# Order of the first two large loads of a decoder trunk: first weight slab ahead of the first norm's scale

## The reference

```python
def rms_norm(x, g):
    y = xf * lax.rsqrt(jnp.mean(xf * xf, axis=-1, keepdims=True) + EPS)
    return (y * g.astype(jnp.float32)).astype(x.dtype)

def swiglu_ffn(x, w_in, w_out):
    gate, up = jnp.split(x @ w_in, 2, axis=-1)
    return (jax.nn.silu(gate) * up) @ w_out

for i in range(DEPTH):
    x = x + 0.5 * swiglu_ffn(rms_norm(x, ffn1_norm[i]), ffn1_w_in[i], ffn1_w_out[i])
    xn = rms_norm(x, mix_norm[i])
    ...
    x = x + y
    x = x + 0.5 * swiglu_ffn(rms_norm(x, ffn2_norm[i]), ffn2_w_in[i], ffn2_w_out[i])
return rms_norm(x, final_norm)
```

## Time and profile before

| | before |
|---|---|
| median of 3 runs | 940.22 us (940.21 to 940.26) |
| span of the profiled execution | 938.5 us |
| TensorE, busy | 927.6 us (99%) |
| TensorE, weight loads | 872.2 us (93%) |
| VectorE, busy | 522.7 us (56%) |
| ScalarE, busy | 411.9 us (44%) |
| GpSimd, busy | 26.7 us (3%) |
| moved by DMA | 170.36 MB, 182 GB/s on average |

### The profile page before, as it was taken

One profiled execution on the slowest core, in us unless ns is written; L12 is line 12 of the kernel. 1 busy time (PEld: TensorE's weight loads), 2 busy tenths in 40 slices (PEclk: granted clock), 3 DMA queues, 4 the chain that ended last, 5 costly groups with the idle time before them and its releaser, 6 DMA issues.

```text
span 938.5 us, 15299 instructions
## 1 busy us (share of the span) xinstructions
PE 927.6 (99%) x6505; PEld 872.2 (93%) x6505; DVE 522.7 (56%) x464; ACT 411.9 (44%) x413; POOL 26.7 (3%) x44
## 2 busy tenths in 40 slices
PE   8999999999999999999999999999999999999997
PEld 7999999989989999999999999999999899999995
DVE  5765545446967665455547444554478475454533
ACT  6453334326744544333435344334364265343322
POOL 1500000000000000000000000000010000000000
PEclk9999999999999999999999999999999999999999
DMA  8985555523512875676518656556184277556501
GB/s 264 310 270 179 179 179 201 196 75 120 172 46 101 303 241 180 217 236 202 179 45 278 217 179 213 184 197 190 46 288 161 90 242 263 185 177 209 196 7 45
DMA packets 124213, 170.36 MB, mean 182 GB/s; under 512 B 2773, under 2 KB 108777, under 8 KB 124168
## 3 DMA queue, kind: packets, MB, share of 16 engines
q1 hardware_dynamic: 124168, 169.69, 54.1%
HBM read 168.63 MB, written 1.05 MB: 181 GB/s over the span
## 4 chain that ended last, share of the span: by engine, by line
PE 96%; issue 1%; DVE 1%; DMA 1%; ACT 1%; POOL 0%; SPq 0%; POOLq 0%; ACTq 0%; DVEq 0%
PE ub L894 10%; PE ub L896 10%; PE ub L895 10%; PE ga L894 10%; PE ga L896 10%; PE ga L895 10%; PE acc L894 10%; PE acc L895 10%; PE acc L896 10%; PE ga L1093 1%; PE tp L955 1%; DMA raw<-in_ffn_w_in_dram 1%; PE ub L1093 1%; PE tp L1180 0%; DVE w_lo L607 0%
## 5 line engine op out<-in xcount | busy, mean ns | idle before, releaser
L607 DVE TENSOR_TENSOR w_lo<-raw,w_hi 128x2048 fp32r<-128x2048 f32 (+1 forms) x154 | 352.1, 2295 | 246.3 <-ACT w_hi L410 246.1
L410 ACT ACTIVATE w_hi<-raw 128x2048 fp32r<-128x2048 f32 (+1 forms) x154 | 292.1, 1902 | 91.9 <-PE acc L896 61.5
L894 PE MATMUL ub<-xn_hi,w_hi 128*128 128x256 f32 x688 | 195.1, 284 | 0.0
L894 PE MATMUL ga<-xn_hi,w_hi 128*128 128x256 f32 x688 | 194.8, 283 | 0.2 <-ACT sgh L455 0.2
L896 PE MATMUL ub<-xn_hi,w_lo 128*128 128x256 f32 x688 | 194.7, 283 | 0.0
L895 PE MATMUL ub<-xn_lo,w_hi 128*128 128x256 f32 x688 | 194.7, 283 | 0.0
L896 PE MATMUL ga<-xn_hi,w_lo 128*128 128x256 f32 x688 | 194.7, 283 | 0.0
L895 PE MATMUL ga<-xn_lo,w_hi 128*128 128x256 f32 x688 | 194.7, 283 | 0.0
L894 PE MATMUL acc<-w_hi,act_hi 128*128 128x512 f32 x416 | 163.6, 393 | 0.0
L895 PE MATMUL acc<-w_lo,act_hi 128*128 128x512 f32 x416 | 162.3, 390 | 0.0
L896 PE MATMUL acc<-w_hi,act_lo 128*128 128x512 f32 x416 | 161.9, 389 | 0.0
(11 more groups left out here) (130 smaller groups left out, 766.0 us busy)
## 6 DMA issues: line engine op xcount, KB each, us to landing
raw<-in_ffn_w_in_dram SPq DMA_DIRECT2D x88, 1024.0 KB, 5.1
raw<-in_ffn_w_out_dram SPq DMA_DIRECT2D x44, 1024.0 KB, 5.0
raw<-in_sgu_w_in_dram SPq DMA_DIRECT2D x8, 1024.0 KB, 5.3
raw<-in_ab_w_in_dram SPq DMA_DIRECT2D x6, 1024.0 KB, 4.9
raw<-in_ab_w_out_dram SPq DMA_DIRECT2D x4, 1024.0 KB, 4.8
raw<-in_sgu_w_out_dram SPq DMA_DIRECT2D x4, 1024.0 KB, 7.1
gain<-in_ffn_norm_dram SPq DMA_DIRECT2D x4, 512.0 KB, 5.8
xres<-in_x_dram SPq DMA_DIRECT2D x2, 512.0 KB, 6.3
```

Of the source, the lines that this page charges most:

```text
L410: act.activation(w_hi[:, n % RING, o:], raw[:, n % RAW, o:], ACT.Copy).then_inc(hi_split, 1)
L607: dve.tensor_tensor(w_lo[:, n % RING, o:], raw[:, n % RAW, o:], w_hi[:, n % RING, o:].bitcast(F32), ALU.subtract).then_inc(lo_split, 1)
L894: pe.matmul(dst, s_hi, m_hi, start=start, stop=False)
```

## The change

SyncE issues the load of slab 0 ahead of the broadcast load of the scale vector. The program of stage 0 is otherwise the same, and so is every other stage, for which `gain_load(0)` isn't called.

```diff
                 if kind == "ffn":
                     wi, wo = in_view(w_in), out_view(w_out)
+                    load(b, wi[:, :, 0:WIDTH])
                     if k == 0:
                         gain_load(0)
-                    load(b, wi[:, :, 0:WIDTH])
                     if k == 0:
                         for t in range(1, TT):
```

## The result

| | before | changed |
|---|---|---|
| median | 940.21 us (939.99 to 940.26, 6 runs) | 943.2 us (942.29 to 943.69, 6 runs) |
| ratio, 95% interval | | 1.0032 (1.0022 to 1.0042) |
| span of the profiled execution | 938.5 us | 941.7 us |
| first matmul into ub (slab 1) | 20.79 | 24.00 |
| span behind that matmul | 917.7 us | 917.7 us |

What follows compares the result with a forecast made beforehand. TensorE, busy 927.6 of 938.5 us, was taken as the bound, so a later start reaches the end whole. Span 938.5 + 2.8 = 941.3, plus 1.72 outside the span, gave 943.0 us; range 941.8 to 944.8.

Steps and rivals of the forecast that it cites:

- The case that was forecast: Start of the kernel: scale lands at 9.4 to 10.7, clock stays; 943.0 us, own range 942.5 to 943.8; chance 0.62.
- the quick scale: Rival on the scale's load: behind slab 0 it lands at 8.8, about +1.7 us, 941.9; chance 0.12.
- the fallen clock: Rival on TensorE: clock falls in the longer gap before the transposes, +0.9 us more, 943.9; chance 0.18.
- The third rival: DMA queue: slab 0 and the scale share the engines evenly, +0.1 to +1.4 us, in the middle 941.0; chance 0.05.
- the start alone counts: TensorE's whole run: a delayed start reaches the end whole; later stages could give back only some 0.4 us.
- step 1: Slab 0's load: lands at 7.5, worth nothing behind ScalarE's xn_hi copies; at most the 0.27 us wait goes.
- step 2: Scale's load behind slab 0: the pair ends where it ended, at 9.87; bounds 8.8 and 10.7.
- the lower bound of 8.8: Scale's landing if it takes 1.3 us, like x's second half, behind a slab that keeps 3.1 us.
- step 3: VectorE and ScalarE: xs starts 3.11 us later, ScalarE reaches slab 0 at 12.65 instead of 9.89, +2.8 us.
- steps 4 to 6: After ScalarE's slab start: the delay passes on to ub (23.6); second warm-up's 0.2 us cost nothing; later loads starve nothing.
- The 0.4 us on slab 1: ScalarE's vanishing slab 1 wait: next xn_hi copy could begin some 0.4 us closer behind its transposes; taken as nothing.
- the clock holds for 4.6 us: TensorE's clock: at the kernel's end it fell 4.6 us after the last instruction; the new gap of 4.4 is shorter.

Runs made afterwards that it cites:

- first warm-up 26: Changed kernel with 26 matmuls instead of 14 in TensorE's first warm-up: 942.73 us.
- slab first in the programs: Changed kernel, warm-ups 26 and 4; slab 0's pieces ahead of the first xn_hi copies on ScalarE, its first piece ahead of the first xn_lo on VectorE: 940.94 us.
- both halves of x first: Kernel before the change, but both loads of x issued first, then the scale, then slab 0: 941.16 us.
- rows not broadcast: Kernel before the change, but the load into the scale's tile reads 128 different rows of x instead of one row 128 times: 939.87 us.
- halves of slab 0: Kernel before the change, slab 0's second piece later in the programs, slab 0 loaded in two halves with x's second half between them: 939.32 us.
- the kernel with the scale as one row: Scale loaded as one 4 KB row and spread over the partitions by TensorE, slab 0 directly behind it, warm-ups 9 + 8 + 4: 944.31 us.

## Why the prediction was right, and where it was not

The time, 943.2, lies 0.2 us from the forecast, and the sign and size hold. The steps do not all hold; two errors cancelled.

**The hit is luck.** The case that was forecast (chance 0.62: scale at 9.4 to 10.7, clock stays) did not come. Two of its rivals came together: the quick scale (0.12, +1.7) and the fallen clock (0.18, +0.9). Both of their signs are in the profile: the first xs starts at 9.06, before 9.2, and the second warm-up takes 5.33 us, more than 3.5. The prediction never priced them together; the sum would have been 940.22 + 1.7 + 0.9 = 942.8. With the clock kept the kernel takes 942.11, below the 942.5 to 943.8 that the forecast case had been given. The third rival, a queue that shares itself between slab 0 and the scale, is out: slab 0 landed alone at 7.45, 3.0 us behind x.

**That the start alone counts: right.** Span less the ub matmul's start:

| kernel | ub at | span | span behind it |
|---|---|---|---|
| before | 20.79 | 938.5 | 917.7 |
| changed | 24.00 | 941.7 | 917.7 |
| changed, again | 23.23 | 940.9 | 917.7 |
| first warm-up 26 | 22.63 | 940.4 | 917.8 |
| slab first in the programs | 21.55 | 939.2 | 917.7 |
| both halves of x first | 21.99 | 939.7 | 917.7 |
| rows not broadcast | 20.58 | 938.3 | 917.7 |
| halves of slab 0 | 19.48 | 937.5 | 918.0 |

The other profiled executions give 917.7 to 918.0 as well. Nothing later gives the delay back; of the 1.3 us that the last kernel gains up to ub, 0.3 are lost again behind it.

**That the early slab is worth nothing (step 1): right,** and shown. It lands at 7.45 as said, is touched at 12.43, and has a value (1.2 us) only where the programs are written otherwise.

**Where the scale lands (step 2): too late by 0.9 us.** "The pair ends where it ended: 9.87" failed. The scale landed at 8.9, next to the lower bound of 8.8. The step took the total of two transfers as fixed whatever the order; but 265 GB/s was neither the time's rate nor a fixed price of the scale. It was that of the scale's row read 128 times behind x, and behind the slab the same load was quicker.

**The delay on ScalarE (step 3): right in mechanism.** With the clock kept, ScalarE reaches slab 0 at 11.75 (the kernel with 26 warm-up matmuls), 1.9 us later than before: the delay of 2.2 us less the 0.27 us wait that it swallowed. By the landing taken it had been 2.8.

**What is hidden (steps 4 to 6): right at full clock.** The 0.4 us on slab 1 brought nothing, and the second warm-up was shielded by the wait of 1.08 us for xs.

**The clock: held for the less likely case, and it came.** It fell in both profiled executions of the changed kernel. The rival's mechanism was right: the longer gap, the slow warm-up, the wait for xs used up. Its price of 0.9 us lies between the 0.6 and the 1.4 found in the two profiled executions, and near the middle of all twelve. The price itself left out a term: the transposes ran at the low level too, 1.94 us instead of 1.23. Against that it took the scale's landing at 9.87, and so a gap of 4.4 us, where it was 3.1. What was wrong was the reading that made it unlikely: that the clock holds for 4.6 us, because that is what it did at the kernel's end. In the gap it fell some 2.3 us after TensorE's last instruction, and 2.6 us in the repeated execution. One such distance is no bound for another, and neither is the length of an idle time: 2.00 us of it left the clock up in one kernel, and in the kernel with the scale as one row it fell 0.2 us after such a wait. The Trainium skill ("TensorE: Matmul & The Clock Gate", Part 1) warns of idle gaps between bursts of matmuls; the trace agrees, with a fall in a gap of 3.1 us, and in the kernel with both halves of x first even after a gap of 1.9 us. There the mean of 0.70 over the stretch from 8.80 to 10.20 puts the fall at 9.4, 2.4 us after the warm-up's end at 6.94, while the transposes that began at 8.80 were running:

```profile
8.80 1.69 PE L954 MATMUL tp<-ident,xs 128*128 128x128 f32 x8 [1.86 <-DVE xs L646]
...
8.80:10.20 1.40, 1.40 (x8) 1.22 (x9) 0.62 (x2) 0.60 (x1) 0.00 (x0) 0.70 1.09 369
```

Part 4 of the same page of the Trainium skill says that transposes in TensorE's transpose mode do not count as busy in the same way. That fits this fall; no run here isolates it.

So the sum that happened is 2.2 - 0.3 = 1.9 us for the scale and, in the profiled executions, 0.6 to 1.4 us for the clock, 2.5 to 3.3; the sum that was written is 2.8 and 0.

## What to carry to other kernels

Before a load is moved ahead of another, look at which of the two is taken up first, and what stands ahead of the other's first use in its engine's program: a transfer that comes early for an engine that is held by a different transfer brings nothing, and the one it overtook comes later by much of its length (the scale by 2.2 us here, where the slab took 3.0). Where the delayed load is what TensorE waits for at the start, count the wait as a gap for the clock too, and look at the spread of the runs: a kernel whose time wanders by a microsecond where it used to stand still may be losing its clock in some of them. The spread alone doesn't show it: the kernel with 26 warm-up matmuls wandered by 1.4 us with its clock and six of its seven spans unchanged, so hold span and mean clock against each other, run by run. And early data became a gain here only where the programs took things up in the order of their landings.

## What the runs showed of the hardware

- One row of 4 KB read 128 times (512 KB written) took 2.4 us as the second transfer of the program, 128 different rows in the same place 1.25 us; behind a slab of 1 MB the former took 1.5 us, behind both loads of x 1.7 us.
- Products over a depth of one row, with 512 columns, took some 0.9 us per instruction (four in 3.78 us) between warm-ups that ran at half speed, the one behind them at 236 ns per instruction instead of 117.
- The granted clock in the rows of stretches reads 1.00 from the start, although the first warm-up takes 5.08 us and the second 3.29 for the same instructions: at the start of a trace the durations have to be believed, not that column.
- The first warm-up's 28 instructions took between 4.97 and 5.84 us in the profiled executions, so its end, and with it the length of the gap behind it, differs from one execution to the next.
- An idle time of 2.00 us left the granted clock at 1.00 in one kernel and was followed by its fall, 2.2 us after the last instruction, in another. The falls in the gap of the changed kernel came 2.3 and 2.6 us after the last instruction, the one at the kernel's end 4.6 us after it.
